# A two-layer transformer: stages that begin on token tile 0, with zero matmuls ahead of three norms' transposes

## The reference

```
def rms_norm(x, g):
    y = x * rsqrt(mean(x * x, axis=-1) + EPS)
    return y * g
def swiglu_ffn(h, w_in, w_out):
    g, u = split(h @ w_in, 2)
    return (silu(g) * u) @ w_out
def memory_cross_attention(h, mem_n, w_q, w_kv, w_o):
    q = h @ w_q ; k, v = split(mem_n @ w_kv, 2)
    p = softmax(q k^T / 16)            # per head
    return (p v) @ w_o
```

## Time and profile before

| | us |
|---|---|
| median of 3 runs | 1749.28 (1747.96 to 1752.64) |
| the profiled execution | 1747.18 |
| its span, first to last instruction | 1745.4 |
| TensorE busy | 1634.2 (94%) |
| VectorE busy | 1036.6 (59%) |
| ScalarE busy | 788.1 (45%) |
| mean granted TensorE clock | 0.978 |

### The profile page before, as it was taken

The page is one execution under the profiler, slowest core; times in us unless marked ns, Lnnn a source line. Parts: engine busy times, 40 slices in busy tenths (PEclk is TensorE's granted clock), DMA queues, the critical chain, the costliest instruction groups (busy, mean ns, idle before and its releaser), DMA issues.

```text
span 1745.4 us, 22031 instructions
## 1 busy us (share of the span) xinstructions
PE 1634.2 (94%) x8513; PEld 1364.8 (78%) x8513; DVE 1036.6 (59%) x1321; ACT 788.1 (45%) x969; POOL 95.4 (5%) x145
## 2 busy tenths in 40 slices
PE   6999987999999999999988899999989999789997
PEld 6788877878888878888985687888778877668886
DVE  4577655567764477745568545554457776564454
ACT  4444343455443343443358444555444455244432
POOL 1000000000100000001000004000010030100000
PEclk9999998999999999999999999999999999899999
DMA  8687744188774477753450234665555531445550
GB/s 307 195 284 241 242 140 169 57 272 273 242 250 159 157 249 271 249 193 91 125 193 1 102 104 138 215 192 186 166 181 202 172 127 63 177 158 192 192 192 24
DMA packets 210198, 311.77 MB, mean 179 GB/s; under 512 B 16538, under 2 KB 145590, under 8 KB 209873
## 3 DMA queue, kind: packets, MB, share of 16 engines
q1 hardware_dynamic: 204112, 288.90, 49.7%
q0 software_dynamic: 6016, 21.94, 3.7%
HBM read 306.59 MB, written 4.21 MB: 178 GB/s over the span
## 4 chain that ended last, share of the span: by engine, by line
PE 82%; DVE 6%; ACT 4%; issue 2%; DMA 1%; POOL 1%; DVEq 1%; PEld 1%; ACTq 1%; PEldq 0%; SPq 0%; POOLq 0%
PE ps L2106 24%; PE ps L2108 24%; PE ps L2107 24%; DVE wlo L1345 2%; PE ps L2251 1%; PE ps L2165 1%; ACT whi L772 1%; DVEq L1328 1%; PE ps L2384 1%; PE ps L2361 1%; PE ps L2172 1%; POOL area L659 1%; DMA area<-in_gate_b 1%; ACT xn L1063 1%; DVE xn L1433 1%
## 5 line engine op out<-in xcount | busy, mean ns | idle before, releaser
L1345 DVE TENSOR_TENSOR wlo<-raw,whi 128x2048 fp32r<-128x2048 f32 x255 | 582.1, 2299 | 248.7 <-ACT whi L772 247.8
L772 ACT ACTIVATE whi<-raw 128x2048 fp32r<-128x2048 f32 x255 | 481.9, 1910 | 183.3 <-PE ps L2108 160.9
L2106 PE MATMUL ps<-wlo,aT_hi 128*128 128x512 f32 (+1 forms) x1280 | 500.6, 391 | 18.3 <-DVE aT_lo L1378 10.6
L2108 PE MATMUL ps<-whi,aT_hi 128*128 128x512 f32 (+1 forms) x1280 | 491.8, 384 | 0.0
L2107 PE MATMUL ps<-whi,aT_lo 128*128 128x512 f32 (+1 forms) x1280 | 491.2, 384 | 0.0
L2106 PEld LDWEIGHTS ps<-wlo,aT_hi 128*128 128x128 f32 x1280 | 242.6, 190 | 68.4 <-issue 15.9
L2108 PEld LDWEIGHTS ps<-whi,aT_hi 128*128 128x128 f32 x1280 | 242.1, 189 | 47.8
L2107 PEld LDWEIGHTS ps<-whi,aT_lo 128*128 128x128 f32 x1280 | 242.7, 190 | 45.9 <-issue 1.2
L2106 PE MATMUL ps<-wlo,hT_hi 128*128 128x512 f32 x480 | 187.8, 391 | 0.0
L2106 PE MATMUL ps<-aT_lo,whi 128*128 128x256 f32 x600 | 174.9, 292 | 13.6 <-ACTq L756 5.0
L2108 PE MATMUL ps<-whi,hT_hi 128*128 128x512 f32 x480 | 187.0, 390 | 0.0
(11 more groups left out here) (317 smaller groups left out, 1256.4 us busy)
## 6 DMA issues: line engine op xcount, KB each, us to landing
raw<-in_ffn_w_in SPq DMA_DIRECT2D x176, 512.0 KB, 4.9
raw<-in_ffn_w_out SPq DMA_DIRECT2D x88, 512.0 KB, 4.4
raw<-in_w_ff SPq DMA_DIRECT2D x64, 512.0 KB, 4.7
raw<-in_ada_w SPq DMA_DIRECT2D x48, 512.0 KB, 5.6
raw<-in_w_in SPq DMA_DIRECT2D x48, 512.0 KB, 4.6
raw<-in_xattn_w_kv SPq DMA_DIRECT2D x32, 512.0 KB, 7.0
raw<-in_xattn_w_q SPq DMA_DIRECT2D x16, 512.0 KB, 5.1
raw<-in_xattn_w_o SPq DMA_DIRECT2D x16, 512.0 KB, 5.9
```

What stands on the lines that cost most here:

```text
L772: act.activation(to, of, ACT.Copy).then_inc(hi_ready[slot], 1)
L1345: dve.tensor_tensor(lo, of, hi, ALU.subtract).then_inc(lo_ready[slot], 1)
L2106: pe.matmul(o, lh, rl, start=start, stop=False, skip_group_check=True)
L2108: return pe.matmul(o, lh, rh, start=False, stop=stop, skip_group_check=True)
```

## The change

Where a stage followed a norm and needed both tiles, it now begins with the products of tile 0 by rows, and tile 1's transposes stand in the middle of them (`rows_from`, `turn_later` at (0, 4)):

- the query's first chunk has form N; 8 transposes of its result (`turn_queries`) and a second pair of copies (`keep_q`) bring it into the old layout;
- the sparse inputs begin with the chunk that had form N already;
- the gated projection transposes the merged rows tile by tile, each as soon as it is summed; the four `sum_parts` come before them and write banks 4 to 7; `sum_parts` 10 and 11 go behind tile 1's transposes of norm 12.

The ten zero matmuls of norms 3, 7 and 8 stand ahead of tile 0's transposes. In the FFNs and the MLP the first piece of round 1's up stands before turn(0), and the rest of round 1 is written out; the FFNs that follow a kv stage take their first pieces in the order of the slabs. In the FFN tails slab 0 of the next stage is split between the two tiles of the last hidden transpose, and slab 1 before x is updated. GpSimd's first `load_ada` moves from the second cross projection to the second query, with other places in `area`.

SyncE and GpSimd (the order of the sparse inputs' slabs; the load of the adaLN sums):

```diff
@@ -444,14 +445,14 @@
     def nsa_inputs(self):
         stages.next()
         w = A["nsa_w_in"][0]
-        for c in range(2):
-            chunk(w, 512 * c, 512, 2 * c)
-        for c, c0 in enumerate((1024, 1280, 1536, 2048)):
-            chunk(w, c0, 256, 2 * (c % 2))
         wv = w.rearrange("(k p) n -> p k n", p=P)
         for s in range(2):
             d = raw[:, s, :].rearrange("p (k h n) -> p k h n", k=4, h=2)
             slab(s, [(d[:, :, h, :], wv[:, 4 * s:4 * s + 4, c0:c0 + 256]) for h, c0 in enumerate((1792, 2304))])
+        for c in range(2):
+            chunk(w, 512 * c, 512, 2 - 2 * c)
+        for c, c0 in enumerate((1024, 1280, 1536, 2048)):
+            chunk(w, c0, 256, 2 - 2 * (c % 2))
         chunk(w, 2560, 48, 2)

     def nsa_compress(self):
...
     def query(self, l):
         enter()
-
-    def cross(self, l):
-        enter()
-
-    def project(self, w, gated=False, part=None):
-        enter()
-        if part == 0:
+        if l:
             pool.memset(ones, 1.0).then_inc(ada_ready, 1)
             self.load_ada(0)
+
```

ScalarE (FFN with norm 4 or 9 ahead of it; its tail; the query; the gated projection). `split(slot)` is the copy of a slab into `whi`:

```diff
-        for begin, end in ((0, 5), (5, rounds - 1)) if mem else ((0, rounds - 1),):
-            if begin:
+        ahead = int(mem or last)
+        if ahead:
+            act.wait_ge(gate_half, fb + 1)
+            act.activation(hs[:, 0, 0:HI], ps[:, 4, 0:HI], ACT.Silu).then_inc(silu_made, 1)
+            split(0, ub[0] + 1)
+            act.wait_ge(consumed[1], db[1] + 1)
+            act.activation(hs[:, 1, 0:HI], ps[:, 5, 0:HI], ACT.Silu).then_inc(silu_made, 1)
+            split(1, ub[1] + 1)
+            second_half(0)
+            split(2, ub[2] + 1)
+            for s in range(3):
+                arrived[s] -= 32
+        for begin, end in ((1, 5), (5, rounds - 1)) if mem else ((ahead, rounds - 1),):
+            if begin == 5:
                 act.wait_ge(mem_in[1], 16 * T)
...
         act.wait_ge(tail_turned, tails.next())
         act.activation(hT_hi[:, 2:4, 0:P], hid[:, 0], ACT.Copy).then_inc(tail_hi, 1)
+        split(0)
         act.wait_ge(hid_turned, fb + rounds)
         act.activation(hT_hi[:, 2:4, P:S], hid[:, 1], ACT.Copy).then_inc(hT_hi_made, 1)
...
-        next_slabs()
+        split(1)
         c_ffn.next(rounds)
...
         def evac(c, b):
-            return act.activation(qT[:, 4 * c:4 * c + 2, :], ps[:, b, :], ACT.Copy, scale=1.0 / 16)
-
-        chunks(2, evac, within=(None, lambda: [self.cross_exps(u) for u in range(4)]))
+            if c == 0:
+                return act.activation(hs[:, 0, :], ps[:, b, :], ACT.Copy)
+            return act.activation(qT[:, 4:6, :], ps[:, b, :], ACT.Copy, scale=1.0 / 16)
+
+        def keep_q(c):
+            if c == 0:
+                act.wait_ge(q_turned, l + 1)
+                act.activation(qT[:, 0:2, :], ps[:, half_of_banks(chunk_no.n - 1), :], ACT.Copy, scale=1.0 / 16)\
+                   .then_inc(q_kept, 1)
+
+        chunks(2, evac, after=keep_q, within=(None, lambda: [self.cross_exps(u) for u in range(4)]))
...
     def project(self, w, gated=False, part=None):
         enter(updates_x=True)
         if gated:
-            turned(range(4))
+            for n in range(4):
+                self.keep_mod(6 + n, 4 + n)
+            turned((2, 3, 6, 7))
         split(2)
         split(3)
-        if gated:
-            for n, bank in enumerate((6, 7, 2, 3)):
-                self.keep_mod(6 + n, bank)
         split(0)
```

VectorE (FFN tail; the query; merge and gated projection; the MLP's first round):

```diff
+        if last:
+            gate_tile(0, 0)
+            split(0, ub[0] + 1)
+            gate_tile(0, 1)
+            split(1, ub[1] + 1)
+            second_half(0)
+            split(2, ub[2] + 1)
+        for begin, end in ((1, 4), (4, rounds - 1)) if last else ((plain, rounds - 1),):
...
         dve.tensor_tensor(hT_lo[:, 2:4, 0:P], hid[:, 0], hT_hi[:, 2:4, 0:P], ALU.subtract).then_inc(tail_made, 1)
+        split(0)
         dve.wait_ge(hT_hi_made, fb + rounds)
         dve.tensor_tensor(hT_lo[:, 2:4, P:S], hid[:, 1], hT_hi[:, 2:4, P:S], ALU.subtract).then_inc(hT_made, 1)
...
-        split(0)
+        split(1)
         dve.wait_ge(half_done, halves.next())
         add(0)
         if last:
             self.weigh_rows(0)
-        split(1)
...
         if gated:
-            for b in range(4):
-                t, k = b // 2, 4 * (b % 2)
-                at = (slice(None), slice(k, k + 4), slice(t * P, (t + 1) * P))
-                lower(b, aT_hi[at], aT_lo[at], ps[:, b, :].rearrange("p (k n) -> p k n", k=4))
-
-        if gated:
+            self.lower_rows((2, 3, 6, 7), (0, 1))
+            split(1)
+            self.lower_rows((2, 3, 6, 7), (2, 3))
             dve.wait_ge(ada_ready, 7)
...
+        if gated:
+            self.scale_gain(12)
         dve.wait_ge(consumed[1], done.n[1])
         add(0, 0)
         add(0, 1).then_inc(dve_evac, 1)
-        if gated:
-            self.scale_gain(12)
         split(0)
         split(1)
...
                     g = bgate[:, t, 1024 * br:1024 * br + 1024]
                     last = dve.tensor_tensor(xn[:, t, :], xn[:, t, :], g, ALU.add)
+                    if br == 2:
+                        last.then_inc(merged, 1)
                 if br == 1:
                     step(last)
         leave()
-        next_slabs()
+        split(0)
...
-        with dve.Fori(0, rounds - 1) as i:
+        self.mlp_tile(0, 0, fb)
+        split(0, ub[0] + 1)
+        self.mlp_tile(0, 1, fb)
+        split(1, ub[1] + 1)
+        self.mlp_turned(0, fb)
+        split(2, ub[2] + 1)
+        split(3, ub[3] + 1)
+        with dve.Fori(1, rounds - 1) as i:
             split(0, ub[0] + i + 1)
```

TensorE (norms and their zero matmuls; the FFN; the query; the projection). The MLP is changed as the FFN is:

```diff
-    def turn_first(self, normed, banks):
+    def turn_first(self, normed, banks, sums=False):
+
+        def second():
+            turn_rows(normed, banks, (2, 3))
+            if sums:
+                sum_parts(10, 6)
+                sum_parts(11, 7)

         turn_rows(normed, banks, (0, 1))
...
         stages.next()
-        if turn:
-            self.turn_first(2 * m, norm_banks(m))
-        if m == 12:
-            pe.wait_ge(mod_kept, 10)
-            sum_parts(10, 6)
-            sum_parts(11, 7)
         if m in (3, 7, 8):
             keep_clock(10, 2 if m == 3 else 7)
+        if turn:
+            self.turn_first(2 * m, norm_banks(m), m == 12)

...
+        ahead = self.later is not None
+
+        def up_part(i, s, t):
+            pe.wait_ge(lo_ready[s], ub[s] + i + 1)
+            h, lw = (w[:, s, :].rearrange("p (k n) -> p k n", k=4) for w in (whi, wlo))
...
+            if t:
+                last.then_inc(consumed[s], 1)
+            elif s:
+                last.then_inc(gate_half, 1)
+
         def up(i):
-            first = type(i) is int and i == 0
-            for s, t in ((0, 0), (1, 0), (0, 1), (1, 1)) if first else ((0, 0), (0, 1), (1, 0), (1, 1)):
...
-                elif first:
+            for s, t in ((0, 0), (0, 1), (1, 0), (1, 1)):
+                up_part(i, s, t)
+
+        def up_first():
+            for s, t in ((0, 0), (1, 0), (0, 1), (1, 1)) if ahead else ((0, 0), (0, 1), (1, 0), (1, 1)):
+                pe.wait_ge(aT_made, rows_ready + 2 * t + s + 1)
+                up_part(0, s, t)
+                if s == t == 0:
                     self.turn_later()
...
+        up_first()

         pe.wait_ge(act_evac, chunk_no.n)
         pe.wait_ge(dve_evac, chunk_no.n)
         for b in range(4):
             pe.matmul(ps[:, b, :], zero[:, 0:P], zero[:, :], start=True, stop=False, skip_group_check=True)
+        pe.wait_ge(hid_made, 2 * fb + 1)
+        up_part(1, 0, 0)
         turn(0)
-        with pe.Fori(1, rounds - 1) as i:
+        up_part(1, 0, 1)
+        up_part(1, 1, 0)
+        up_part(1, 1, 1)
+        down(0)
+        turn(1)
+        with pe.Fori(2, rounds - 1) as i:
             up(i)
             down(i - 1)
             turn(i)
...
     def query(self, l):
-        self.turn_later()
-        enter()
-        chunk(0, 512, turned(bank()))
-
-        def scores():
+        stages.next()
+        b = bank()
+        chunk(0, 512, rows(b), between={(0, 4): self.turn_later}, rows_from=c_turned.n - 4)
+
+        def turn_queries():
             pe.wait_ge(act_evac, chunk_no.n - 1)
             pe.wait_ge(dve_evac, chunk_no.n - 1)
+            for k in range(4):
+                for t in range(T):
+                    c = S * (k % 2) + P * t
+                    last = pe.transpose(ps[:, b + k // 2, c:c + P], hs[:, t, P * k:P * k + P], ident)
+            last.then_inc(q_turned, 1)
+
+        def scores():
+            pe.wait_ge(q_kept, 2 * (l + 1))
             for u in range(4):
                 self.cross_score(u)

-        chunk(2, 512, turned(bank()), between={(1, 0): scores})
+        chunk(2, 512, turned(bank()), between={(0, 4): turn_queries, (1, 0): scores})

...
     def project(self, w, gated=False, part=None):
+        stages.next()
         if gated:
-            enter()
-            turn_rows()
-            pe.wait_ge(aT_made, c_turned.next(4))
+            pe.wait_ge(branch_kept, 5)
```

(43 more changed lines are left out.)

163 lines of the change are left out of this document (96 added, 67 removed).

## The result

The changed kernel takes 1727.32 us (median of 4 runs, 1723.65 to 1728.36), the kernel before, run beside it, 1750.96 (4 runs, 1747.96 to 1753.4). The ratio is 0.9862, with a 95% interval of 0.9839 to 0.9885: 24 us, or 1.4%, faster. The forecast was 1718.4 within 1710 to 1729. The time lies in the range, 9 us above the forecast.

The account below looks back on a forecast made before the run. TensorE was taken as the bound, idle at stage borders. Terms 3.1 + 1.3 + 1.5 + 5.6 + 4.2 + 6.5 + 0.9 + 1.8 + 6.0 = 30.9 us off 1747.2 gave 1716.3; 2.1 more for the median, 1718.4, range 1710 to 1729.

Parts of the forecast that it names:

- the tails: Slabs split earlier in the FFN tails: 1.3 us gained at the pool stage, 1.5 at the head, 5.6 at second kv.
- norm 3 and the query: First query after norm 3 starts on tile 0: 5.1 us gained, less 0.9 for new transposes, so 4.2.
- norm 7: Norm 7 and sparse inputs: zeros fill idle time and keep the clock up, tile 0 starts first; 6.5 us gained.
- the lost wait for the sums: At the projection, TensorE's wait for the adaLN additions goes: 1.8 us gained.
- the gated projection: Sums move into TensorE's wait and tile 0 starts first: 6.0 us gained, after adding 2.5 for an expected clock fall.
- The moved load: GpSimd's adaLN additions move to the second query: 0.9 us of new wait there, 1.8 of wait gone at the projection.
- the prediction's sentence on the exclusive lock: In the second query, a VectorE split may stand behind one whole GpSimd addition, making that step's net about 0.
- the 15 that the prediction had named as its sign: The prediction is wrong if TensorE's total idle time does not fall by over 15 us.
- Rival 1: The clock falls in new idle times, 2 to 2.5 us at four places, about 9: 1727 us; chance 0.15.
- the step of the first rounds: FFN and MLP: a piece of round 1 covers TensorE's wait for the gate product; 3.1 us gained (1 to 5.5).
- the fourth rival: Zeros at norms 3 and 7 delay the work as at norm 8: 4.7 us more, 1723; chance 0.06.
- Rivals 2 and 3: 2: borders win only the first piece, 1726, chance 0.08. 3: TensorE waits for instructions, 1789, 0.06 including other new stalls.

## Why the prediction was nearly right

*What held.* The bound (TensorE, and only its borders), the tails (2.3, 1.3 and 5.2 against 1.3, 1.5 and 5.6), norm 3 and the query, norm 7, the lost wait for the sums, and the gated projection (7.1 against 6.0; the clock fell at its first piece as written, and took some 1.5 of the 2.5 us added for it: 13.76 from 1496.06 to the evacuation, where 12.3 was the sum at full clock). The moved load came out at +0.6 in all, some 2.0 of wait less 1.5 in and behind the query; I had forecast 1.8 less 0.9. The step rested on 1.3 of room in the softmax chain, and there was less than the split needed: at its place VectorE's split took 4.37 instead of 2.29 while GpSimd added, and TensorE waited 1.64 instead of 0.92 behind it. So the prediction's sentence on the exclusive lock held. TensorE's idle time fell by 24.3, over the 15 that the prediction had named as its sign.

*What failed.* First, the sum itself: it left every untouched stage at the time of before. Rival 1 named the clock, priced it at 9, and put it into new idle times; the loss of 11.5 lies in stages that the change only moved in time, behind idle times that were there before and behind one row of narrow products. The sum also counted what the clock would give back at the borders (some 2.5 in the second keys and values) and nothing that it could take elsewhere. The runs that show it: the same kernel again (the falls repeat), fourteen zeros at one of these idle times (8.9 us back in the three stretches), a shift by zeros that fill nothing (4.3 less in the three stretches), and the old tails (4.8 less). Second, the step of the first rounds: TensorE's new order brings 0.4 in all, not 3.1; the ffn1 stages gave 3.0 without it, and that the whole came near the forecast size is luck. Third, norm 7: the zeros cost about 1 and keep up nothing, since the wait they were to fill had shrunk to 1.23. With norm 8's 2.3 they cost some 3.3; the fourth rival, which charged 4.7 for norms 3 and 7, was right at one of them and too dear. Rivals 2 and 3 are out: the borders gave what was summed, and no issue time appeared at the first rounds.

*The comparison itself* held a trap. The profiled execution of before was one of the fastest of its kernel (1747.2; its medians are 1749.6 to 1753.7), so the gain by medians, 24, is larger than by the traces, 19.9.

*Open.* What decides whether the clock falls behind a given idle time. The same waits ahead of the projection gave 24.35 us at 952.26 and at 972.97, 27.5 to 27.6 at 952.95, 957.09, 958.06 and 959.97, and 26.2 at 958.15 (the start of the projection in seven kernels' traces, each with its own history ahead). The place in time counted from the kernel's start doesn't decide it either (958.06 and 958.15). I have no rule that fits all of them. Also open is what made the 3.0 us of the two ffn1 stages.
